# Rotating retention's queries and keys as channels by tokens, and issuing the first attention's scores one slot sooner

## The chip, the cores and the metric

One NeuronCore of a Trainium2 chip. The metric is the time of one execution in microseconds (us). All times of "before" are of the same kernel; lower is better.

## What is computed

One layer of an encoder on 512 tokens of width 1024, in float32: a norm, one projection `h @ w_in`, two mixers side by side, an output projection, a second norm, a router and 16 gated experts, a last norm. What matters here is the second mixer, retention: 4 heads with 128 channels. Its queries and keys are rotated by position and then multiplied with each other:

```python
def rotary(t):                      # t (B,S,H,D)
    half = D // 2
    ang = arange(S)[:, None] * inv[None]
    t1, t2 = t[..., :half], t[..., half:]
    return concatenate([t1 * cos - t2 * sin, t1 * sin + t2 * cos], axis=-1)

qr, kr = rotary(qb), rotary(kb) * 128 ** -0.5
o_b = chunkwise_retention(qr, kr, vb)          # scores need channels on the contracted axis
```

The first mixer is a windowed attention (8 heads of 64 channels, 2 key heads) with a softmax over 192 keys.

## The kernel before, in words

TensorE, VectorE (DVE), ScalarE (ACT), GpSimd (POOL) and the DMA queue SP each run a list of instructions in order; semaphores tie them together.

**Slots.** The projections are a walk over weight groups `g` and tiles `t` (line 74, `STEPS`). Group 0 to 2 give the first attention's queries, keys and values, groups 3 to 10 retention's (3, 4 and 7, 8: queries and keys of a pair of heads; 5, 6 and 9, 10: values and gates), groups 11 to 14 the output projection. A step is called slot `k = (g - 3) * 4 + t`. In each slot TensorE does one tile: 12 matmuls of 512 columns into PSUM bank `t` (`tile_product`, line 1760; every product is a triple of high and low parts, L1577 to L1579). Behind the tile stand small pieces of the mixers, by hand-written slot lists (lines 79 to 94): on TensorE in the order values, transposed probabilities, scores, retention's values, retention's scores, transposes of the rotated tiles (lines 1802 to 1824). ACT and DVE walk the same slots in lists of their own (lines 859 to 914 and 1303 to 1361) and end each slot with a quarter of the split of a weight group that is needed two groups later (L744 or L740 on ACT makes the high part, L1054 or L1049 on DVE the low part).

**First attention.** Eight units `u`, two for each token tile. `scores(u)` (line 1650) writes banks 4 and 5, so for `u` over 0 it waits for `logit_ready` to be `u`: DVE has read the scores of unit `u - 1`. On DVE slot `2u` does, in this order, `softmax_denom(u - 1)` (L1141, L1142, L1144; its last instruction releases `turn_prob(u - 1)`), `attention_out` in some slots (L1151, waits for `values`), `softmax_logits(u)` (L1126 to L1135; its last instruction, L1135, is `logit_ready`). ACT does the exponentials (L806) in slot `2u + 1`, in every case after it has copied the transposed probabilities of unit `u - 1` (L813). TensorE does `scores(u)` in slot `2u`, `turn_prob(u)` (8 transposes, 4 for `u` under 2) in slot `2u + 3` (line 1669), `values` in slots 6, 10, 14, 18.

**Rotation.** Tile `n` (0 to 3 the first pair of heads, 4 to 7 the second) stands in its bank as tokens by channels. `rotate(n)` (line 1153) reads it twice (L1168, L1169: times cosine, times sine) and joins the halves (L1170, L1171) into SBUF; `turn_rot(n)` (line 1694) turns it with 4 transposes on TensorE in slots 6, 8, 10, 12, 22, 23, 25, 26; ACT's `copy_rot(n)` (L817) brings it back into `qkb_t`, channels by tokens. TensorE's tiles of groups 5 and 9 write the same banks again, so tile `t` of group 9 waits for `rot_ready` to be `4 + t + 1` (line 1783). `retention_scores` (L1714), `retention_mask` (L1182, L1185), `retention_values` (L1728) and `retention_out` (L1198 to L1210) follow.

`turn` (L1584) is the helper of all transposes.

Of the kernel before, what the change touches and what calls it, by code (L numbers as in the profile page):

```python
# [17 lines left out]
P = 128  # L18
# [60 lines left out]
TURN_V_SLOT = 1  # L79
SCORE_SLOTS = tuple(range(0, 16, 2))  # L80
DENOM_SLOTS = tuple(range(2, 18, 2))
TURN_SLOTS = tuple(range(3, 19, 2))
VALUE_SLOTS = tuple(range(6, 22, 4))
ROTATE_SLOTS = (5, 7, 7, 9, 20, 22, 23, 25)
ROT_SLOTS = (6, 8, 10, 12, 22, 23, 25, 26)
ROT_BANKS = (7, 7, 7, 7, 5, 6, 5, 6)
RET_SCORE_SLOTS = (18, 20, 27, 29)
# [9 lines left out]
EARLY = 2  # L97
QK_LAST, VG_LAST = (4, 8), (6, 10)
SCM_OFF = (0, 512, 896, 1152)
# [4 lines left out]
def log_gamma(h):  # L104
    return math.log(1.0 - 2.0 ** (-5.0 - h))
# [9 lines left out]
def tile_value(g, t):  # L115

    return STEPS.index((g, t)) + 1 + T if g else t + 1
# [17 lines left out]
def build(nc, x, norm1_g, w_in, attn_sinks, rel_bias, ret_gn_g, w_out, norm2_g, rg_w, rg_b, re_w, re_b,  # L135
          w_gate, w_up, w_down, final_g, table, out):
    ctx = ExitStack()
    with ctx:
# [8 lines left out]
        def sem(name):  # L147
            return ctx.enter_context(nc.semaphore(name))
# [31 lines left out]
        def region(o, n):  # L180
            return arena[:, o:o + n]
# [16 lines left out]
        decay = region(O_DECAY, 1024).rearrange("p (h j) -> p h j", h=B_HEADS)  # L198
        rot = [region(O_ROT, 512), region(O_MIX + 2 * D, 512)]
        rot_b = region(O_TMP, 512)  # L200
        v_t = region(O_ROT, 512)
        cos = region(O_COS, 256).rearrange("p (t c) -> p t c", t=T)
        sin = region(O_COS + 256, 256).rearrange("p (t c) -> p t c", t=T)
        gn_g = region(O_GN, 512)
# [84 lines left out]
        sq_done, root_done, h_ready, h_turned, h_hi, h_lo = (sem(n) for n in ("sq_done", "root_done", "h_ready", "h_turned", "h_hi", "h_lo"))  # L289
        qkv_copied, v_turned, va_copied = sem("qkv_copied"), sem("v_turned"), sem("va_copied")  # L290
        dve_step, act_step = sem("dve_step"), sem("act_step")
# [3 lines left out]
        sink_exp, p_scaled = sem("sink_exp"), sem("p_scaled")  # L295
        rot_ready, rot_turned, rot_copied = sem("rot_ready"), sem("rot_turned"), sem("rot_copied")
        v_copied, gate_copied, silu_done, g_ready = (sem(n) for n in ("v_copied", "gate_copied", "silu_done", "g_ready"))
# [425 lines left out]
        def _(act):  # L723
# [90 lines left out]

            def copy_rot(n):
                act.wait_ge(rot_turned, n + 1)
                nc.scalar.copy(qkb_t[:, :, n % T * P:(n % T + 1) * P],  # L817
                               ps[:, ROT_BANKS[n], :].rearrange("p (b s) -> p b s", b=4)).then_inc(rot_copied, 1)

# [39 lines left out]
            for g, t in STEPS:  # L859
# [11 lines left out]
                if k == TURN_V_SLOT:  # L871
                    act.wait_ge(v_turned, 1)
                    nc.scalar.copy(region(O_VA, 512), ps[:, 7, :]).then_inc(va_copied, 1)
# [12 lines left out]
                if k in MIX_A_SLOTS:  # L886
                    mix_hi(0, [t])
                if k in ROT_SLOTS:
                    copy_rot(ROT_SLOTS.index(k))
                if k in EXP_SLOTS:  # L890
# [143 lines left out]
        def _(dve):  # L1034
# [118 lines left out]
            def rotate(n):  # L1153

                t = n % T
                v = ps[:, t, :].rearrange("p (h a c) -> p h a c", a=2, c=B_DIM // 2)
                own = rot[n % 2 if n < T else 0]
                ra = own.rearrange("p (h a c) -> p h a c", a=2, c=B_DIM // 2)
                rb = rot_b.rearrange("p (h a c) -> p h a c", a=2, c=B_DIM // 2)
                dve.wait_ge(mm_done, tile_value(QK_LAST[n // T], t))  # L1160
                if n:
                    dve.wait_ge(rot_ready, n)
                if n >= 2:
                    dve.wait_ge(rot_turned, n if n >= T else n - 1)
                cs = cos[:, t, :].unsqueeze(1).to_broadcast([P, 8, 64])
                sn = sin[:, t, :].unsqueeze(1).to_broadcast([P, 8, 64])
                v8 = ps[:, t, :].rearrange("p (h c) -> p h c", c=64)
                nc.vector.tensor_tensor(own.rearrange("p (h c) -> p h c", c=64), v8, cs, ALU.mult)  # L1168
                step_done(nc.vector.tensor_tensor(rot_b.rearrange("p (h c) -> p h c", c=64), v8, sn, ALU.mult))  # L1169
                nc.vector.tensor_tensor(ra[:, :, 0, :], ra[:, :, 0, :], rb[:, :, 1, :], ALU.subtract)  # L1170
                nc.vector.tensor_tensor(ra[:, :, 1, :], ra[:, :, 1, :], rb[:, :, 0, :], ALU.add).then_inc(rot_ready, 1)  # L1171

            def retention_mask(i):

                gamma_p = math.exp(log_gamma(i) * P)
                dve.wait_ge(rs_ready, i + 1)
                if i:
                    dve.wait_ge(ro_ready, i)
                for kt in range(T):
                    bank, c0 = ((4, 0), (5, 0), (6, 0), (6, 256))[kt]  # L1180
                    near = min(2, T - kt) * P
                    ins = nc.vector.tensor_tensor(scm[:, SCM_OFF[kt]:SCM_OFF[kt] + near], ps[:, bank, c0:c0 + near],  # L1182
                                                  decay[:, i, 0:near], ALU.mult)
                    for far in range(2, T - kt):
                        ins = nc.vector.scalar_tensor_tensor(  # L1185
                            scm[:, SCM_OFF[kt] + far * P:SCM_OFF[kt] + (far + 1) * P],
                            ps[:, bank, c0 + far * P:c0 + (far + 1) * P], gamma_p ** (far - 1),
                            decay[:, i, P:2 * P], ALU.mult, ALU.mult)
                ins.then_inc(scm_ready, 1)
# [384 lines left out]
        def _(pe):  # L1574
# [89 lines left out]
            def turn_v():  # L1664

                pe.wait_ge(qkv_copied, 8)
                turn(7, [v_t[:, t * P:(t + 1) * P] for t in range(T)]).then_inc(v_turned, 1)

            def turn_prob(u):
                if u:  # L1670
                    pe.wait_ge(pt_copied, probs_value(u - 1))
                if u >= 2:
                    pe.wait_ge(mix_a, u // 2)
                turned = sum(slot < TURN_SLOTS[u] for slot in ROT_SLOTS[:T])
                if turned:
                    pe.wait_ge(rot_copied, turned)
                pe.wait_ge(p_scaled, u + 1)
                for b in range(1 if u < 2 else 0, 2):
                    ins = turn(6 + b, [prob[u % 2][:, hh // 2, hh % 2, b * P:(b + 1) * P] for hh in range(4)])
                ins.then_inc(p_turned, 1)  # L1680
# [12 lines left out]

            def turn_rot(n):
                pe.wait_ge(rot_ready, n + 1)
                if n < T:
                    pe.wait_ge(pt_copied, probs_value(TURN_SLOTS.index(ROT_SLOTS[n] - 1)))
                elif n < T + 2:
                    pe.wait_ge(scm_ready, 2)
                else:  # L1700
                    pe.wait_ge(rot_copied, n - 1)
                own = rot[n % 2 if n < T else 0]
                turn(ROT_BANKS[n], [own[:, i * P:(i + 1) * P] for i in range(4)]).then_inc(rot_turned, 1)

            def retention_scores(i):
                pe.wait_ge(rot_copied, T * (i // 2 + 1))
                if i:
                    pe.wait_ge(scm_ready, i)
                if i == 2:
                    pe.wait_ge(mix_b, 2)  # L1710
                for kt in range(T):
                    bank, c0 = ((4, 0), (5, 0), (6, 0), (6, 256))[kt]
                    n = (T - kt) * P
                    ins = nc.tensor.matmul(ps[:, bank, c0:c0 + n], qkb_t[:, 2 + i % 2, kt * P:(kt + 1) * P],  # L1714
                                           qkb_t[:, i % 2, kt * P:], start=True, stop=True)
                ins.then_inc(rs_ready, 1)
# [43 lines left out]
            def tile_product(g, t):  # L1760
# [17 lines left out]
                else:  # L1778
# [15 lines left out]
                    for k in range(4):  # L1794
                        kk = 4 * half + k
                        ins = triple(ps[:, t, :], ht_hi[:, kk, tok], ht_lo[:, kk, tok],
                                     as_chunks(hi(g))[:, k, :], as_chunks(lo(g))[:, k, :],
                                     half == 0 and k == 0, half == 1 and k == 3)
# [3 lines left out]
            for g, t in STEPS:  # L1802
# [6 lines left out]
                if k in TURN_SLOTS:  # L1809
                    turn_prob(TURN_SLOTS.index(k))  # L1810
                if k in SCORE_SLOTS:
                    scores(SCORE_SLOTS.index(k))
                if k in RET_VALUE_SLOTS:
                    retention_values(RET_VALUE_SLOTS.index(k))
                if k in RET_SCORE_SLOTS:
                    retention_scores(RET_SCORE_SLOTS.index(k))
                if k in ROT_SLOTS:
                    turn_rot(ROT_SLOTS.index(k))
                if k == MIX_B_SLOT:
# [256 lines left out]
```

## Time and profile before

| | us |
|---|---|
| median of 3 runs (548.21 to 549.0) | 548.93 |
| the profiled execution | 548.88 |
| span of its trace | 547.1 |
| TensorE busy in the span | 535.0 (98%) |
| DVE busy in the span | 420.3 (77%) |
| ACT busy in the span | 353.9 (65%) |

The mixers take the stretch from 49 to 192 us of the span; the experts the time from about 247 us to the end. A busy TensorE is not one at its peak: the end of a matmul is modelled, so what tells its pace is the distance from start to start. In rows of the timeline the bracket at the end is idle time ahead of the row and what ended it.

### The profile page before, as it was taken

Reading aid. Unit: us, or ns where it says so; the run is one execution under the profiler, and the core shown is the slowest. Engines: PE = TensorE matmul, PEld = TensorE weight load, DVE = VectorE, ACT = ScalarE, POOL = GpSimd, SP = SyncE. Lnnn points to the kernel's source line nnn. Section 1 sums busy time; section 2 is a strip of 40 time slices with the busy share of each in tenths; the row PEclk is TensorE's granted clock in tenths of the full one; section 3 lists DMA queues with packets and bytes.
Section 4 is the critical chain, followed back from the end, with each engine's and each line's share of the span. In section 5 each row is a group of like instructions: output and inputs, shape, how many; then the busy total and the mean of one; then the engine's idle time right before and its main releaser. Section 6 shows DMA issues by size and latency. Waiting matters only on the chain.

```text
span 547.1 us, 7888 instructions
## 1 busy us (share of the span) xinstructions
PE 535.0 (98%) x2685; PEld 438.7 (80%) x2686; DVE 420.3 (77%) x572; ACT 353.9 (65%) x474; POOL 96.3 (18%) x117
## 2 busy tenths in 40 slices
PE   7999999999999999999999999999999999999994
PEld 5988777777877888898878888888888888888883
DVE  5563599564865853388999889898989898898986
ACT  5563654770226263356877887888787887888745
POOL 3260000000000000034330224122221222110520
PEclk8999999999999999999999999999999999999998
DMA  8999122323020236658999999999999999999894
GB/s 318 374 288 401 44 75 78 77 79 76 2 78 0 78 115 228 236 211 277 399 380 377 373 380 395 375 375 365 381 363 364 373 385 382 371 393 396 264 211 177
DMA packets 63739, 143.78 MB, mean 263 GB/s; under 512 B 3811, under 2 KB 13339, under 8 KB 63584
## 3 DMA queue, kind: packets, MB, share of 16 engines
q1 hardware_dynamic: 56528, 120.24, 61.7%
q0 software_dynamic: 7040, 22.66, 13.5%
q10 hardware_dynamic: 144, 0.52, 0.3%
q8 instruction: 15, 0.25, 0.2%
q14 instruction: 12, 0.10, 0.0%
HBM read 132.51 MB, written 14.30 MB: 268 GB/s over the span
## 4 chain that ended last, share of the span: by engine, by line
PE 88%; DVE 6%; ACT 2%; issue 2%; DMA 1%; ACTq 0%; POOL 0%; DVEq 0%; POOLq 0%
PE ps L1577 25%; PE ps L1579 24%; PE ps L1578 24%; PE ps L1584 7%; DVE lo_ring L1366 2%; PE ps L1728 2%; PE ps L1714 2%; PE ps L1690 1%; PE ps L1660 1%; PE ps L1755 1%; DMA arena<-norm_g 1%; PE ps L1845 1%; DVE act_lo L1064 0%; ACT arena L762 0%; ACT hi_ring L744 0%
## 5 line engine op out<-in xcount | busy, mean ns | idle before, releaser
L1366 DVE TENSOR_TENSOR lo_ring<-arena,hi_ring 128x2048 fp32r<-128x2048 f32 x94 | 213.8, 2288 | 24.7 <-ACT hi_ring L925 24.7
L1577 PE MATMUL ps<-hi_ring,act_hi 128*128 128x512 f32 x576 | 230.0, 399 | 0.3 <-DVE act_lo L1217 0.2
L1579 PE MATMUL ps<-hi_ring,act_lo 128*128 128x512 f32 x576 | 224.9, 390 | 0.0
L1578 PE MATMUL ps<-lo_ring,act_hi 128*128 128x512 f32 x576 | 224.3, 389 | 0.0
L925 ACT ACTIVATE hi_ring<-arena 128x2048 fp32r<-128x2048 f32 x94 | 180.2, 1917 | 26.7 <-PE ps L1579 26.7
L1579 PEld LDWEIGHTS ps<-hi_ring,act_lo 128*128 128x128 f32 x576 | 108.1, 188 | 23.3
L1577 PEld LDWEIGHTS ps<-hi_ring,act_hi 128*128 128x128 f32 x576 | 108.2, 188 | 22.9 <-issue 1.6
L1578 PEld LDWEIGHTS ps<-lo_ring,act_hi 128*128 128x128 f32 x576 | 108.4, 188 | 20.8
L1054 DVE SCALAR_TENSOR_TENSOR lo_ring<-arena,over,hi_ring 128x512 fp32r<-128x512 f32 x40 | 29.3, 748 | 29.4 <-ACT hi_ring L744 29.2
L1064 DVE TENSOR_TENSOR act_lo<-ps,act_hi 128x512 fp32r<-128x512 f32 x56 | 36.8, 683 | 6.4 <-ACT act_hi L777 5.9
L1584 PE MATMUL ps<-keep,arena 128*128 128x128 f32 x260 | 35.2, 275 | 1.2 <-DVE arena L1074 0.7
L631 POOL DMA_INDIRECT arena<-h_dram,gather_idx x12 | 30.9, 2575 | 20.3 <-issue 20.3
L1584 PEld LDWEIGHTS ps<-keep,arena 128*128 128x128 f32 x260 | 29.3, 140 | 5.5 <-issue 1.9
L637 POOL DMA_INDIRECT y_dram<-y,row_info x14 | 15.6, 1112 | 95.1 <-issue 95.1
L561 POOL DMA_DIRECT2D arena<-norm_g x1 | 0.6, 556 | 153.9 <-PE ps L1584 153.9
L744 ACT ACTIVATE hi_ring<-arena,over 128x512 fp32r<-128x512 f32 x40 | 27.5, 718 | 0.1
L1577 PE MATMUL ps<-act_hi,hi_ring 128*128 128x256 f32 (+1 forms) x64 | 22.4, 349 | 0.1
L1579 PE MATMUL ps<-act_hi,lo_ring 128*128 128x256 f32 (+1 forms) x64 | 21.8, 340 | 0.0
L1578 PE MATMUL ps<-act_lo,hi_ring 128*128 128x256 f32 (+1 forms) x64 | 21.8, 340 | 0.0
L945 ACT ACTIVATE act_hi<-ps 128x512 fp32r<-128x512 f32 x15 | 9.0, 601 | 18.7 <-PE ps L1584 18.7
L930 ACT ACTIVATE act_hi<-ps 128x512 fp32r<-128x512 f32 x32 | 17.3, 592 | 5.8 <-PE ps L1845 4.1
L962 ACT ACTIVATE y<-ps,row_info 128x512 f32<-128x512 f32 x28 | 19.0, 679 | 3.1 <-PE ps L1579 3.1
(242 smaller groups left out, 518.4 us busy)
## 6 DMA issues: line engine op xcount, KB each, us to landing
arena<-w_gate SPq DMA_DIRECT2D x32, 1024.0 KB, 16.7
arena<-w_up SPq DMA_DIRECT2D x32, 1024.0 KB, 17.6
arena<-w_down SPq DMA_DIRECT2D x32, 1024.0 KB, 15.2
arena<-w_in SPq DMA_DIRECT2D x16, 512.0 KB, 7.3
y_dram<-arena POOLq DMA_DIRECT2D x8, 512.0 KB, 11.2
res<-y_dram POOLq DMA_DIRECT2D x8, 512.0 KB, 9.7
arena<-w_in SPq DMA_DIRECT2D x2, 1024.0 KB, 10.7
arena<-w_out SPq DMA_DIRECT2D x4, 512.0 KB, 6.4
```

Source lines behind the costliest of these rows:

```text
L631: by_length(e, lambda n: pool.indirect_dma_start(x_rows[b][0:n, :], None, h2_dram, bass.IndirectOffsetOnAxis(ap=gather_idx[0:n, b:b + 1], ...
L744: ins = nc.scalar.activation(dst, src, ACT.Copy, scale=gain)
L925: nc.scalar.activation(hi(N1 + n12), raw(n12), ACT.Copy).then_inc(hi_done, 1)
L930: nc.scalar.activation(xt[b][0][:, 4 * a:4 * a + 4, :], ps[:, 4 + a, :].rearrange("p (k s) -> p k s", k=4), ACT.Copy).then_inc(x_hi, 1)
L962: nc.scalar.activation(y_buf[b][:, a * 512:(a + 1) * 512], ps[:, 2 + a, :], ACT.Copy, scale=row_info[:, 4 * b + 2:4 * b + 3].bitcast(F32)) ...
L1054: ins = nc.vector.scalar_tensor_tensor(dst, src, gain, src_hi.bitcast(F32), ALU.mult, ALU.subtract)
L1064: nc.vector.tensor_tensor(dst, ps[:, bank, :].rearrange("p (k s) -> p k s", k=4), src_hi.bitcast(F32), ALU.subtract).then_inc(done, 1)
L1366: nc.vector.tensor_tensor(lo(N1 + n12), raw(n12), hi(N1 + n12).bitcast(F32), ALU.subtract).then_inc(lo_done, 1)
L1577: nc.tensor.matmul(dst, a_hi, b_hi, start=start, stop=False)
L1578: nc.tensor.matmul(dst, a_hi, b_lo, start=False, stop=False)
L1579: return nc.tensor.matmul(dst, a_lo, b_hi, start=False, stop=stop)
L1584: ins = nc.tensor.transpose(ps[:, bank, i * P:(i + 1) * P], blk, ident)
```

## The change

Weights and activations change roles in groups 3, 4, 7 and 8: bank `t` now holds channel block `t` (two query heads, two key heads) by 512 tokens, so the result needs no transposes. The rotation pairs channel c with c + 64, that is, partitions: ACT copies the two halves of the bank crosswise into SBUF (`swap_halves`), DVE multiplies the bank by a cosine table into `qkb_t`, the swapped copy by a signed sine table, and adds. The tables must stand as channels by tokens: they are turned once on TensorE (`turn_cos`, slot -4) and spread by eight ACT copies; the cosine table moves once (slot 16), because its first place is needed for retention's scores. `turn_rot` and `copy_rot` are gone. TensorE issues `scores(u)` in slots 0, 1, 3, 5, ..., 13, behind the transposes of that slot; the slots of DVE and ACT for the first attention stay.

```diff
 SCORE_SLOTS = tuple(range(0, 16, 2))
+PE_SCORE_SLOTS = (0,) + tuple(range(1, 15, 2))
-ROTATE_SLOTS = (5, 7, 7, 9, 20, 22, 23, 25)
-ROT_SLOTS = (6, 8, 10, 12, 22, 23, 25, 26)
-ROT_BANKS = (7, 7, 7, 7, 5, 6, 5, 6)
+SWAP_SLOTS = (4, 6, 6, 8, 20, 21, 22, 23)
+ROTATE_SLOTS = (5, 7, 7, 9, 21, 22, 23, 25)
+COS_MOVE_SLOT = 16
...
-            def copy_rot(n):
-                act.wait_ge(rot_turned, n + 1)
-                nc.scalar.copy(qkb_t[:, :, n % T * P:(n % T + 1) * P],
-                               ps[:, ROT_BANKS[n], :].rearrange("p (b s) -> p b s", b=4)).then_inc(rot_copied, 1)
+            def spread(f, dst):
+                dims = dst.rearrange("p (i a s) -> p i a s", i=2, a=2)
+                both = ps[:, 6, 2 * f * P:2 * (f + 1) * P].rearrange("p (i s) -> p i s", i=2)
+                for a in range(2):
+                    for half in range(2):
+                        nc.scalar.activation(dims[half * 64:(half + 1) * 64, :, a, :], both[a * 64:(a + 1) * 64, :, :], ACT.Copy,
+                                             scale=-1.0 if f and half == 0 else 1.0).then_inc(cos_set, 1)
+            def swap_halves(n):
+                bank, own = n % T, swap[n % 2]
+                act.wait_ge(mm_done, tile_value(QK_LAST[n // T], bank))
+                if n >= 2:
+                    act.wait_ge(rot_ready, n - 1)
+                for half in range(2):
+                    nc.scalar.copy(own[half * 64:(half + 1) * 64, :],
+                                   ps[(1 - half) * 64:(2 - half) * 64, bank, :]).then_inc(swapped, 1)
...
+                if (g, t) == (NA - 1, 2):
+                    act.wait_ge(rel_out, 16)
+                    act.wait_ge(cos_v_turned, 1)
+                    spread(0, cos_t[0])
+                if k == 0:
+                    spread(1, sin_t)
+                if k == COS_MOVE_SLOT:
+                    act.wait_ge(s_ready, 2 * T)
+                    nc.scalar.copy(cos_t[1], cos_t[0]).then_inc(cos_set, 1)
...
             def rotate(n):
-                dve.wait_ge(mm_done, tile_value(QK_LAST[n // T], t))
...
+                dve.wait_ge(mm_done, tile_value(QK_LAST[pair], block))
+                dve.wait_ge(cos_set, 8 + pair)
+                if pair:
+                    dve.wait_ge(rs_ready, 2)
+                nc.vector.tensor_tensor(turned, ps[:, block, :], cos_t[pair], ALU.mult)
+                dve.wait_ge(swapped, 2 * n + 2)
+                step_done(nc.vector.tensor_tensor(own, own, sin_t, ALU.mult))
+                nc.vector.tensor_tensor(turned, turned, own, ALU.add).then_inc(rot_ready, 1)
...
-            def turn_rot(n):
...
+            def turn_cos():
+                pe.wait_ge(cos_in, 4 * 16)
+                turn(6, [region(O_COS + i * P, P) for i in range(4)]).then_inc(cos_v_turned, 1)
             def retention_scores(i):
-                pe.wait_ge(rot_copied, T * (i // 2 + 1))
+                pe.wait_ge(rot_ready, T * (i // 2 + 1))
...
+                        if g in QK:
+                            ins = triple(ps[:, t, :], as_chunks(hi(g))[:, k, tok], as_chunks(lo(g))[:, k, tok],
+                                         ht_hi[:, kk, :], ht_lo[:, kk, :], half == 0 and k == 0, half == 1 and k == 3)
+                            continue
...
-                if k in SCORE_SLOTS:
-                    scores(SCORE_SLOTS.index(k))
+                if k in PE_SCORE_SLOTS:
+                    scores(PE_SCORE_SLOTS.index(k))
-                if k in ROT_SLOTS:
-                    turn_rot(ROT_SLOTS.index(k))
+                if (g, t) == (NA - 1, 0):
+                    turn_cos()
```

## Rows read from the trace of the kernel before

**Rows 1.** The page, chain of work that ended last, shares by engine

```profile
PE 88%; DVE 6%; ACT 2%; issue 2%; DMA 1%; ACTq 0%; POOL 0%; DVEq 0%; POOLq 0%
```

**Rows 2.** Busy time by stretch: PE, PEld, DVE, ACT, POOL, granted clock, DMA share, GB/s

```profile
49.00:119.00 70.00, 69.76 (x369) 52.44 (x367) 50.82 (x115) 41.12 (x118) 0.00 (x0) 1.00 0.28 86
119.00:192.00 73.00, 72.25 (x362) 57.74 (x363) 47.55 (x129) 23.94 (x45) 0.00 (x0) 1.00 0.19 58
```

**Rows 3.** TensorE's timeline, start, busy us: transposes that go, and tiles around them

```profile
74.25 0.66 PE L1584 MATMUL ps<-keep,arena 128*128 128x128 f32 x4
74.66 0.47 PE L1577 MATMUL ps<-hi_ring,act_hi 128*128 128x512 f32 x1
...
139.55 0.39 PE L1577 MATMUL ps<-hi_ring,act_hi 128*128 128x512 f32 x1
...
142.27 2.39 PE L1728 MATMUL ps<-arena 128*128 128x128 f32 x20
...
153.92 0.66 PE L1584 MATMUL ps<-keep,arena 128*128 128x128 f32 x4 [0.17 <-DVE arena L1171]
154.34 0.47 PE L1577 MATMUL ps<-hi_ring,act_hi 128*128 128x512 f32 x1
```

**Rows 4.** TensorE's timeline, slots 3 to 6, 9, 13: transposes, scores, tiles

```profile
62.50 0.48 PE L1577 MATMUL ps<-hi_ring,act_hi 128*128 128x512 f32 x1
...
65.41 0.92 PE L1660 MATMUL ps<-arena 64*128 64x192 f32 x8
...
69.47 0.47 PE L1577 MATMUL ps<-hi_ring,act_hi 128*128 128x512 f32 x1
...
85.43 1.06 PE L1584 MATMUL ps<-keep,arena 128*128 128x128 f32 x8
86.25 0.48 PE L1577 MATMUL ps<-hi_ring,act_hi 128*128 128x512 f32 x1
...
102.96 1.03 PE L1584 MATMUL ps<-keep,arena 128*128 128x128 f32 x8
```

**Rows 5.** DMA queue and POOL: the last table that turn_cos waits for

```profile
arena<-ret_gn_g POOLq DMA_DIRECT2D x1, 256.0 KB, 8.9
...
18.13 0.54 POOL L540 DMA_DIRECT2D arena<-ret_gn_g  x1
```

**Rows 6.** DVE's timeline: ends of softmax_logits 1, 2, 4, 6, end of softmax_denom 3

```profile
63.85 0.16 DVE L1135 TENSOR_TENSOR norm_tmp<-sinks,norm_tmp 128x4 f32<-128x4 f32 x1
...
70.56 0.16 DVE L1135 TENSOR_TENSOR stat<-sinks,stat 128x4 f32<-128x4 f32 x1
...
84.33 0.96 DVE L1144 TENSOR_TENSOR arena<-arena,norm_tmp 128x768 f32<-128x768 f32 x1
...
87.64 0.17 DVE L1135 TENSOR_TENSOR stat<-sinks,stat 128x4 f32<-128x4 f32 x1
...
104.17 0.16 DVE L1135 TENSOR_TENSOR stat<-sinks,stat 128x4 f32<-128x4 f32 x1
```

**Rows 7.** Groups by shape, 60 to 210 us: busy us, mean ns, idle before

```profile
L1168 DVE TENSOR_TENSOR arena<-ps,arena 128x512 f32<-128x512 f32 x8 | 5.5, 688 | 3.5 <-PE ps L1579 2.3 <-PE ps L1584 1.1
L1170 DVE TENSOR_TENSOR arena<-arena 128x256 f32<-128x256 f32 x8 | 3.4, 426 | 0.3
L1210 DVE TENSOR_TENSOR arena<-arena 128x512 f32<-128x512 f32 x4 | 2.8, 692 | 0.1
```

**Rows 8.** ACT's timeline: two half-height copies out of PSUM, in slot -3

```profile
44.39 1.19 ACT L869 COPY arena<-ps 64x512 f32<-64x512 f32 x2
```

**Rows 9.** DVE's timeline, second pair: the wait for a free bank, and rotate(6)'s end

```profile
145.24 0.69 DVE L1168 TENSOR_TENSOR arena<-ps,arena 128x512 f32<-128x512 f32 x1 [1.13 <-PE ps L1584]
...
153.45 0.42 DVE L1171 TENSOR_TENSOR arena<-arena 128x256 f32<-128x256 f32 x1
```

**Rows 10.** Busy time by stretch at the start, columns as in rows 2

```profile
5.00:10.00 5.00, 3.48 (x15) 2.00 (x15) 3.82 (x9) 3.06 (x6) 0.37 (x1) 0.97 1.04 385
10.00:15.00 5.00, 4.87 (x22) 3.38 (x21) 3.88 (x8) 4.82 (x10) 0.00 (x0) 0.69 1.04 388
```

More of the change, by code:

```diff
@@ L97 @@
 EARLY = 2
-QK_LAST, VG_LAST = (4, 8), (6, 10)
+QK, QK_LAST, VG_LAST = (3, 4, 7, 8), (4, 8), (6, 10)
 SCM_OFF = (0, 512, 896, 1152)
@@ L198, in build @@
         decay = region(O_DECAY, 1024).rearrange("p (h j) -> p h j", h=B_HEADS)
-        rot = [region(O_ROT, 512), region(O_MIX + 2 * D, 512)]
-        rot_b = region(O_TMP, 512)
+        swap = [region(O_ROT, 512), region(O_TMP, 512)]
         v_t = region(O_ROT, 512)
-        cos = region(O_COS, 256).rearrange("p (t c) -> p t c", t=T)
-        sin = region(O_COS + 256, 256).rearrange("p (t c) -> p t c", t=T)
+        cos_t = [region(O_SCM, 512), region(O_QA, 512)]
+        sin_t = region(O_COS, 512)
         gn_g = region(O_GN, 512)
@@ L289, in build @@
         sq_done, root_done, h_ready, h_turned, h_hi, h_lo = (sem(n) for n in ("sq_done", "root_done", "h_ready", "h_turned", "h_hi", "h_lo"))
-        qkv_copied, v_turned, va_copied = sem("qkv_copied"), sem("v_turned"), sem("va_copied")
+        qkv_copied, cos_v_turned, va_copied = sem("qkv_copied"), sem("cos_v_turned"), sem("va_copied")
         dve_step, act_step = sem("dve_step"), sem("act_step")
@@ L295, in build @@
         sink_exp, p_scaled = sem("sink_exp"), sem("p_scaled")
-        rot_ready, rot_turned, rot_copied = sem("rot_ready"), sem("rot_turned"), sem("rot_copied")
+        rot_ready, swapped, cos_set = sem("rot_ready"), sem("swapped"), sem("cos_set")
         v_copied, gate_copied, silu_done, g_ready = (sem(n) for n in ("v_copied", "gate_copied", "silu_done", "g_ready"))
@@ L871, in _ @@
                 if k == TURN_V_SLOT:
-                    act.wait_ge(v_turned, 1)
+                    act.wait_ge(cos_v_turned, 2)
                     nc.scalar.copy(region(O_VA, 512), ps[:, 7, :]).then_inc(va_copied, 1)
@@ L887, in _ @@
                     mix_hi(0, [t])
-                if k in ROT_SLOTS:
-                    copy_rot(ROT_SLOTS.index(k))
+                if (g, t) == (NA - 1, 2):
[7 more added lines that the diff above has]
+                    nc.scalar.copy(cos_t[1], cos_t[0]).then_inc(cos_set, 1)
+                for n, slot in enumerate(SWAP_SLOTS):
+                    if slot == k:
+                        swap_halves(n)
                 if k in EXP_SLOTS:
@@ L1153, in rotate @@
             def rotate(n):
[L1155 to L1159, printed above, removed]
-                dve.wait_ge(mm_done, tile_value(QK_LAST[n // T], t))
[L1161 to L1171, printed above, removed]
+                pair, block = n // T, n % T
+                own, turned = swap[n % 2], qkb_t[:, block, :]
+                dve.wait_ge(mm_done, tile_value(QK_LAST[pair], block))
[6 more added lines that the diff above has]
+                nc.vector.tensor_tensor(turned, turned, own, ALU.add).then_inc(rot_ready, 1)
             def retention_mask(i):
                 gamma_p = math.exp(log_gamma(i) * P)
+                dve.wait_ge(cos_set, 9)
                 dve.wait_ge(rs_ready, i + 1)
@@ L1666, in turn_v @@
                 pe.wait_ge(qkv_copied, 8)
-                turn(7, [v_t[:, t * P:(t + 1) * P] for t in range(T)]).then_inc(v_turned, 1)
+                turn(7, [v_t[:, t * P:(t + 1) * P] for t in range(T)]).then_inc(cos_v_turned, 1)
             def turn_prob(u):
@@ L1673, in turn_prob @@
                     pe.wait_ge(mix_a, u // 2)
-                turned = sum(slot < TURN_SLOTS[u] for slot in ROT_SLOTS[:T])
-                if turned:
-                    pe.wait_ge(rot_copied, turned)
                 pe.wait_ge(p_scaled, u + 1)
@@ L1692, in values @@
                 ins.then_inc(o_ready, 1)
-            def turn_rot(n):
[L1695 to L1703, printed above, removed]
+            def turn_cos():
+                pe.wait_ge(cos_in, 4 * 16)
+                turn(6, [region(O_COS + i * P, P) for i in range(4)]).then_inc(cos_v_turned, 1)
             def retention_scores(i):
-                pe.wait_ge(rot_copied, T * (i // 2 + 1))
+                pe.wait_ge(rot_ready, T * (i // 2 + 1))
                 if i:
@@ L1816, in _ @@
                     retention_scores(RET_SCORE_SLOTS.index(k))
-                if k in ROT_SLOTS:
-                    turn_rot(ROT_SLOTS.index(k))
+                if (g, t) == (NA - 1, 0):
+                    turn_cos()
                 if k == MIX_B_SLOT:
```

## The prediction

> **What bounds the kernel now.** I read the chain of waits first: 88% of it is TensorE, so what TensorE issues or waits for is the time [rows 1]. The table by stretch comes next: in the mixers (49 to 192 us) TensorE is busy 69.8 of 70 us and 72.3 of 73, at full clock, while the DMAs do little (shares of 0.28 and 0.19) [rows 2]. That says that nothing stands ahead of TensorE, but not by how much: DVE is busy 51 of the first 70 us, and it and ACT feed TensorE in each slot. So I read the timelines of both side by side, for how long before its use each result of DVE is there. For a transfer or an engine behind the mixers I found nothing that would absorb a shift: each later load and split waits for a count that TensorE's tiles set, so a microsecond lost or won in the mixers is one at the end. The sum is made against the profiled execution, 548.88 us (span 547.1 and 1.8 around it), and that is within 0.05 of the median, 548.93.
>
> **What leaves and enters TensorE's list.** A tile that nothing interrupts takes 2.72 us from start to start (139.55 to 142.27) [rows 3]. One that follows small pieces and is followed by scores takes 2.91 (62.50 to 65.41) [rows 4], so an interruption costs 0.19 beside its own work. A `turn_rot` takes 0.41 (74.25 to 74.66) [rows 3].
> - First pair: four `turn_rot`, in slots that keep other pieces or lose their scores too: 4 x 0.41 = 1.6 less.
> - Second pair: four `turn_rot`, three of them alone in their slot: 4 x 0.41 + 3 x 0.19 = 2.2 less.
> - Scores in odd slots, which the transposes interrupt anyway: slots 2, 4, 8 and 12 become whole. 4 x 0.19 = 0.8 less. Their own work moves and stays.
> - `turn_cos`: 0.41 and most of an interruption, 0.5 more. It waits for four tables; the last is issued at 18.1 and lands 8.9 us later, at 27 [rows 5], and TensorE comes to it in slot -4, ahead of the copies that ACT makes in slot -3 at 44.4 [rows 8]. So no wait.
> - The query and key tiles with the roles changed: the same number of matmuls of 512 columns and as many weight loads. The nearest rows are the same shape, so 0, with 0.02 a tile either way as bounds.
>
> All of it: 4.1 us less, if TensorE never waits. That is the gain on offer.
>
> **The scores' new wait.** `scores(u)` needs `softmax_logits(u - 1)` finished on DVE. In slot `2u` it had a whole tile more time. Where it stands now is where the next tile starts in the rows, behind the transposes of slot `2u - 1`; I set the end of the logits against it:
> - u = 2: TensorE is there at 62.5 [rows 4], the logits end at 63.85 + 0.16 = 64.0 [rows 6]. 1.5 late.
> - u = 3: 69.5 against 70.7. 1.25 late. u = 5: 86.25 against 87.8. 1.55 late. u = 7: 102.96 + 0.8 = 103.75 against 104.3. 0.6 late [rows 4, 6].
> - u = 1, 4 and 6 read off in the same way come out at 0, 0.2 late and 0.3 early.
>
> These don't add up as they stand: a wait gives DVE time for the next, and a shorter list takes time from it. So I went through slots 1 to 17 in order with the distances of the rows.
> - u = 2: slot 2 is 0.2 shorter, so 1.6 to 1.7 us of wait. Then slot 4 is whole, and TensorE reaches the transposes of slot 5 1.4 later than before. ACT copies these and then does the exponentials, so both are late, by 0.9 net of ACT's own slack, and DVE with them (it has almost no idle time from 66 to 96 us).
> - u = 3: DVE's logits and TensorE are now level: 0.1. u = 4: 0.3.
> - u = 5: `turn_prob(3)` waited for `softmax_denom(3)` already before: it ends at 84.33 + 0.96 = 85.3 and the transposes start at 85.43 [rows 4, 6]. DVE does the logits of unit 4 right behind that denominator, 2.5 us (85.3 to 87.8), and TensorE's transposes take 0.8 (85.43 to 86.25). So whenever DVE is the late one here, the scores wait 2.5 - 0.8 = 1.7. This holds however much the list shrinks.
> - Behind that wait on TensorE stand tile 10 and `values(1)`; DVE's `attention_out(1)` waits for these, and `softmax_logits(5)` for it. So DVE gets about 2 us later, and at u = 7 the wait is 1.3 to 1.4 instead of 0.6.
>
> Together 1.6 + 0.1 + 0.3 + 1.7 + 1.4 and twice 0.1 at the denominators = 5.3 us. Slots 1 to 17 save 1.6 + 0.8 = 2.4 (0.1 more is in gaps that close). Net +2.8 at slot 18. The last wait there, `turn_prob(7)` for its denominator, has no piece that changes and stays.
>
> **The second pair.** `rotate(4)` stood in slot 20 on DVE, in time that was idle; it now needs `retention_scores(1)` done and stands behind `retention_out(0)`. DVE's path from there to the end of `rotate(6)` loses the 1.1 us wait for a free bank [rows 9] and takes in a whole rotation of about 2 us. A rotation itself: before two passes of 0.688 and two of 0.42, after three of 0.69, which is 0.15 less [rows 7]; over three of them 0.4. So `rotate(6)` ends at 153.87 + 2.0 - 1.1 - 0.4 = 154.3. TensorE's tile 26 waits for it, because it writes the bank that `rotate(6)` reads, and before it started at 154.34, behind transposes that had waited for DVE too [rows 3]. So the 2.2 us that TensorE saves turn into a wait at tile 26 (1.7 to 2.0) and tile 27 (0.4). Net 0, I take +0.1.
>
> **ACT.** Eight copies of 0.59 go, sixteen of half height come: a pair takes 1.19 [rows 8], so the height saves nothing and ACT has about 5 us more, with 3 us for the eight spreads (in slots -2 and 0) and 0.6 for the move of the cosine table. The swaps wait for a tile that ACT used to wait for a slot later, and behind them stand only splits that are due two groups on. ACT is busy 41 of 70 us [rows 2]. Cost 0; if the swap of slot 4 pushed the exponentials of slot 5, it would be up to 0.5. The lower bound, that copies freed of `turn_rot` let the exponentials start sooner, is -0.3.
>
> **Sum.** +0.5 (`turn_cos`) + 2.8 + 0.1 = +3.4. 548.9 + 3.4 = 552.3 us. A measurement here can tell about 0.2% (1.1 us) from no change, so this is slower.
>
> **A rule against the change.** At the start TensorE is busy 3.5 of 5 us, and in the 5 us after that the granted clock is 0.69, so some 60% of them passed at the lower of its two levels, which cost 1.5 us [rows 10]. The new waits of 1.4 to 1.7 us stand alone in some 7 us of full work each, so I expect the clock to stay; it is a rival below. The Trainium skill, TensorE: Matmul & The Clock Gate, "Part 1: The HAM clock gate", says that the throttled clock is the default and that activity is what releases it. By that rule the waits could cost more than their length; the rows at the start agree with it, and no row of the mixers shows it.
>
> **The rivals.**
> - *TensorE stays the bound and the transposes' time is won.* Place: `scores(2)` and `scores(5)`, and tile 26. Price: -4.1 if none of them waits, 544.8 us; faster. For it: 98% busy, and 88% of the chain. It decides at the logits: they would have to end 1.6 us sooner, against a DVE list that the change shortens by 0.15 for each rotation only. Against it: rows 6. Chance 0.11.
> - *The first attention's waits are half as long* (ACT freed of copies that waited for `turn_rot`, or a part that I counted twice): +0.5 + 0.1 + 0.2 to 1.0 gives 549.7 to 550.5, and with a gain of 1 us in the second pair 548.7 at the least. Chance 0.14.
> - *The clock falls behind the waits*: once or twice 1.5 us on top, 553.8 to 555. Chance 0.08.
> - *As summed*: 551.2 to 553.4. Chance 0.67.
>
> **How the numbers follow.** The likeliest is 552.3. The range takes in the half-length case from 549.2 and one fall of the clock, 554.0; it leaves out about 0.17. Faster by over 0.2%: the first rival and nearly nothing else, 0.12. Within 0.2% (547.8 to 550.0): most of one half of the second, 0.08. Slower: 0.80.
>
> **What would show it.** After: `scores` rows with an idle bracket that names L1135's line on DVE, some 1.6 us at unit 2, 1.7 at unit 5, 1.4 at unit 7, little at 3, 4 and 6; an idle bracket of nearly 2 us before the third tile of group 9 that names the rotation's last add; slot 18 about 3.3 us later than before, and slot 36 about 3.4; the experts' stretch as long as before. I am wrong if the logits of units 1 and 4 end sooner than here against the transposes, if tile 26 doesn't wait, if rotations take over 2.2 us each (an SBUF add dearer than 0.69), or if granted clocks under 1 appear after 49 us.

## The result: slower by 0.6%, and the profile after

The changed kernel takes 551.74 us (median of 4 runs, 551.45 to 552.32) against 548.57 before (548.13 to 549.0): ratio 1.0058, 95% interval 1.0039 to 1.0077, so 3.2 us more. The profiled execution took 551.84 us, span 550.1.

TensorE's waits from 26 to 215 us of the changed kernel come first (who waited at which line, for whom and whose line: us in total, times, longest). L1678 is `scores`, L1595 the first matmul of a tile, L1602 the transposes; L1159 on DVE is the last instruction of the logits, L1188 the last of a rotation.

```profile
PE ps L1678 <- DVE stat L1159: 2.2, 2, 1.3
PE ps L1595 <- DVE arena L1188: 1.8, 2, 1.7
PE ps L1678 <- DVE norm_tmp L1159: 1.4, 1, 1.4
PE ps L1737 <- issue: 0.5, 1, 0.5
PE ps L1602 <- DVE arena L1168: 0.3, 1, 0.3
```

The first three are new; a sixth, of 0.2, was there before as well. TensorE's timeline of the changed kernel places them (start, busy us; the bracket is idle time ahead of the row):

```profile
40.57 0.60 PE L1602 MATMUL ps<-keep,arena 128*128 128x128 f32 x4
40.92 0.47 PE L1595 MATMUL ps<-act_hi,hi_ring 128*128 128x512 f32 x1
...
52.00 0.71 PE L1678 MATMUL ps<-arena 64*128 64x128 f32 x8
...
62.26 0.65 PE L1602 MATMUL ps<-keep,arena 128*128 128x128 f32 x4
64.33 0.92 PE L1678 MATMUL ps<-arena 64*128 64x192 f32 x8 [1.42 <-DVE norm_tmp L1159]
...
78.95 1.03 PE L1602 MATMUL ps<-keep,arena 128*128 128x128 f32 x8
79.92 0.92 PE L1678 MATMUL ps<-arena 64*128 64x192 f32 x8
...
86.39 1.03 PE L1602 MATMUL ps<-keep,arena 128*128 128x128 f32 x8
88.75 0.92 PE L1678 MATMUL ps<-arena 64*128 64x192 f32 x8 [1.33 <-DVE stat L1159]
...
97.32 1.03 PE L1602 MATMUL ps<-keep,arena 128*128 128x128 f32 x8
...
106.65 0.92 PE L1678 MATMUL ps<-arena 64*128 64x192 f32 x8 [0.86 <-DVE stat L1159]
...
127.66 2.42 PE L1723 MATMUL ps<-arena 128*128 128x512 f32 x8
...
157.50 0.50 PE L1595 MATMUL ps<-hi_ring,act_hi 128*128 128x512 f32 x1 [1.66 <-DVE arena L1188]
160.69 0.50 PE L1595 MATMUL ps<-hi_ring,act_hi 128*128 128x512 f32 x1 [0.17 <-DVE arena L1188]
...
194.96 1.91 PE L1602 MATMUL ps<-keep,arena 128*128 128x128 f32 x16
```

`scores(2)`, `scores(5)` and `scores(7)` wait 1.42, 1.33 and 0.86 us; tile 26, the third of group 9, waits 1.66 and tile 27 0.17. The same places on DVE's timeline:

```profile
60.44 0.75 DVE L1078 SCALAR_TENSOR_TENSOR lo_ring<-arena,over,hi_ring 128x512 fp32r<-128x512 f32 x1 [4.05 <-ACT hi_ring L744]
...
64.02 0.16 DVE L1159 TENSOR_TENSOR norm_tmp<-sinks,norm_tmp 128x4 f32<-128x4 f32 x1
...
85.13 0.96 DVE L1168 TENSOR_TENSOR arena<-arena,norm_tmp 128x768 f32<-128x768 f32 x1
...
88.45 0.16 DVE L1159 TENSOR_TENSOR stat<-sinks,stat 128x4 f32<-128x4 f32 x1
...
94.54 0.69 DVE L1175 COPY arena<-ps 128x512 f32<-128x512 f32 x1 [1.26 <-PE ps L1705]
...
101.97 0.75 DVE L1078 SCALAR_TENSOR_TENSOR lo_ring<-arena,over,hi_ring 128x512 fp32r<-128x512 f32 x1 [3.56 <-ACT hi_ring L744]
...
156.75 0.69 DVE L1188 TENSOR_TENSOR arena<-arena 128x512 f32<-128x512 f32 x1
```

The logits of unit 1 end at 64.18 and `scores(2)` starts at 64.33; those of unit 4 end at 88.61, `scores(5)` starts at 88.75. The denominator of unit 3 (L1168) ends at 86.09 and its logits 2.5 us later, while the transposes between take 0.8. At 94.54 the lateness comes back to DVE: DVE idles 1.26 us for `values(1)`, which stands on TensorE behind the wait at `scores(5)` (these rows answer to [rows 6]). The rows at 60.44 and 101.97 are DVE's shares of the weight splits in slots 1 and 11. Ahead of them DVE idles 4.05 and 3.56 us for ACT, so its list is full ahead of `scores(5)`, but not ahead of `scores(2)` and `scores(7)`.

The mixers fall into two parts, by three marks on TensorE's timeline: start of `scores(0)`, start of `retention_scores(0)` in slot 18, start of the transposes of the mixed rows in slot 35. For the changed kernel these are the rows at 52.00, 127.66 and 194.96; for the other kernels the numbers are read off in the same way.

| kernel | scores(0) | first part, to slot 18 | second part, to slot 35 | span |
|---|---|---|---|---|
| before | 51.83 | 72.86 | 67.16 | 547.1 |
| after | 52.00 | 75.66 | 67.30 | 550.1 |
| scores back | 52.32 | 71.77 | 67.36 | 546.6 |
| scores early alone | 51.91 | 76.32 | 67.14 | 550.4 |
| retention_out(1) later | 55.31 | 75.68 | 64.88 | 551.0 |
| both edits | 51.50 | 71.78 | 64.88 | 543.2 |
| two early | 52.01 | 71.76 | 67.33 | 546.3 |
| less DVE work | 52.10 | 75.32 | 67.31 | 549.8 |

Between before and after the first part has 2.80 us more and the second 0.14. With 0.17 ahead of `scores(0)` and 0.1 less behind slot 35 that is the 3.0 of the spans.

### The profile page after: what moved, and what is told of

The parts are those of the page before. It is cut to its first block, busy times and chain, and to the rows that moved or that the text cites. A ratio compares the mean times of both kernels' runs of the same rounds, so it can differ in the third digit from the quotient of the medians.

```text
span 550.1 us, 7836 instructions
## 1 busy us (share of the span) xinstructions
PE 532.6 (97%) x2657; PEld 436.3 (79%) x2658; DVE 419.6 (76%) x564; ACT 362.9 (66%) x491; POOL 96.5 (18%) x117
## 4 chain that ended last, share of the span: by engine, by line
PE 80%; DVE 11%; ACT 4%; issue 3%; DMA 1%; ACTq 0%; POOL 0%; DVEq 0%; POOLq 0%
PE ps L1595 23%; PE ps L1597 22%; PE ps L1596 22%; PE ps L1602 6%; DVE lo_ring L1384 2%; PE ps L1723 2%; PE ps L1737 1%; ACT arena L806 1%; PE ps L1764 1%; PE ps L1705 1%; DMA arena<-norm_g 1%; PE ps L1858 1%; DVE lo_ring L1078 1%; DVE arena L1185 1%; DVE arena L1150 1%
## 5 line engine op out<-in xcount | busy, mean ns | idle before, releaser
L1595 PE MATMUL ps<-hi_ring,act_hi 128*128 128x512 f32 x512 | 204.0, 398 | 2.1 <-DVE arena L1188 1.8
L1597 PE MATMUL ps<-hi_ring,act_lo 128*128 128x512 f32 x512 | 199.9, 390 | 0.0
L1596 PE MATMUL ps<-lo_ring,act_hi 128*128 128x512 f32 x512 | 199.5, 390 | 0.0
L1595 PEld LDWEIGHTS ps<-hi_ring,act_hi 128*128 128x128 f32 x512 | 96.2, 188 | 25.6 <-issue 3.7
L1596 PEld LDWEIGHTS ps<-lo_ring,act_hi 128*128 128x128 f32 x512 | 96.3, 188 | 18.8
L1595 PE MATMUL ps<-act_hi,hi_ring 128*128 128x512 f32 (+1 forms) x128 | 48.0, 375 | 0.1
L1597 PE MATMUL ps<-act_hi,lo_ring 128*128 128x512 f32 (+1 forms) x128 | 46.5, 363 | 0.0
L1596 PE MATMUL ps<-act_lo,hi_ring 128*128 128x512 f32 (+1 forms) x128 | 46.5, 363 | 0.0
L1602 PE MATMUL ps<-keep,arena 128*128 128x128 f32 x232 | 31.2, 278 | 0.8 <-DVE arena L1098 0.5
L1602 PEld LDWEIGHTS ps<-keep,arena 128*128 128x128 f32 x232 | 27.0, 143 | 3.3 <-DVE arena L1098 0.9
L1595 PEld LDWEIGHTS ps<-act_hi,hi_ring 128*128 128x128 f32 x128 | 24.1, 189 | 6.3 <-issue 1.8
L1597 PEld LDWEIGHTS ps<-act_hi,lo_ring 128*128 128x128 f32 x128 | 24.1, 188 | 3.9
L1596 PEld LDWEIGHTS ps<-act_lo,hi_ring 128*128 128x128 f32 x128 | 24.2, 189 | 3.4
```

What stands on the lines that cost most here:

```text
L1595: nc.tensor.matmul(dst, a_hi, b_hi, start=start, stop=False)
L1596: nc.tensor.matmul(dst, a_hi, b_lo, start=False, stop=False)
L1597: return nc.tensor.matmul(dst, a_lo, b_hi, start=False, stop=stop)
L1602: ins = nc.tensor.transpose(ps[:, bank, i * P:(i + 1) * P], blk, ident)
```

## The experiments

**Scores back.** One line of the changed kernel; TensorE's scores stand in the even slots again.

```diff
-PE_SCORE_SLOTS = (0,) + tuple(range(1, 15, 2))
+PE_SCORE_SLOTS = SCORE_SLOTS
```

> The changed kernel with the first attention's scores back in TensorE's slots 0, 2, ..., 14. Theory (the loss is TensorE waiting at scores(2), scores(5) and scores(7) for DVE's logits of the unit before): these waits (1.4 + 1.3 + 0.9 us) and the 0.2 us ahead of scores behind transposes go, four interruptions of 0.2 come back, and the first pair's 1.6 us of transposes show, but for a wait of about 0.6 at turn_prob(3): 3.3 to 3.8 us less than the changed kernel, 547.9 to 548.5, level with the kernel before (ratio 0.999). The waits at tile 26 and 27 stay. Rival (the rotation's new list on DVE and ACT makes the loss, wherever the wait shows): the waits move to the transposed probabilities, and it stays over 550.5.

Measured: 547.8 us (10 runs) against 548.66 for the kernel before, of which there were 19 runs beside these experiments (ratio 0.9983, 0.9974 to 0.9993). The first part is 3.9 us shorter than in the changed kernel, and its waits are these (columns as above):

```profile
PE ps L1595 <- DVE arena L1188: 1.9, 2, 1.7
PE ps L1602 <- DVE arena L1168: 0.7, 2, 0.4
PE ps L1737 <- issue: 0.5, 1, 0.5
PE ps L1595 <- DVE act_lo L1235: 0.2, 1, 0.2
```

No score waits. The wait at `turn_prob(3)` that the theory wanted is the 0.4 in the second row; the other 0.3 in it is `turn_prob(7)`. The waits did not move elsewhere, so the rival falls, and the time is slightly below the range that I gave. So the rotation alone is a small gain, 0.9 us.

**Scores early alone.** The other half: the kernel before, with the scores moved and nothing else.

```diff
+PE_SCORE_SLOTS = (0,) + tuple(range(1, 15, 2))
...
-                if k in SCORE_SLOTS:
-                    scores(SCORE_SLOTS.index(k))
+                if k in PE_SCORE_SLOTS:
+                    scores(PE_SCORE_SLOTS.index(k))
```

> The kernel before with nothing changed but TensorE's scores in slots 0, 1, 3, ..., 13. Theory: waits of 1.4 to 1.6 us at scores(2), 0.9 to 1.3 at scores(5), 0.6 at scores(7), each kept to the end: 2.9 to 3.3 us slower than before, 551.5 to 551.9. Rival (the rotation makes the loss): 548 to 549, as before, or up to 0.5 faster for the interruptions saved.

Measured: 552.23 us (ratio 1.0065, 1.0048 to 1.0082), 3.6 us more than before, nearly all of it in the first part (+3.46). The loss is there without the new rotation, so the rival falls. But 552.23 is above the range that I gave, while the waits at `scores(5)` and `scores(7)`, 0.79 and 0.40, are shorter than I expected.

```profile
PE ps L1661 <- DVE norm_tmp L1136: 1.4, 1, 1.4
PE ps L1661 <- DVE stat L1136: 1.2, 2, 0.8
```

The idle time at the scores is 2.6 us, less than the 3.46. One reason is a gap that I had not priced: scores behind transposes start 0.17 to 0.18 us after the transposes would let a tile start. It shows at 78.95 in the changed kernel: eight transposes take 0.79 when a tile follows (115.22 to 116.01 in the changed kernel; 0.82 from 85.43 to 86.25 before [rows 4]), and 0.97 when scores do (78.95 to 79.92). The other reason is that a bracket starts at the modelled end of the transposes, 0.24 to 0.3 us behind the point where a tile would start. Counted from that point, TensorE loses 1.72, 1.02 and 0.65 us at units 2, 5 and 7, and 0.17 or 0.18 at each of the other four, 4.1 in all. Two interruptions saved (slots 2 and 4) are 0.4, and slots 8 and 12, where `turn_rot` still stands, give 0.1 each: 4.1 - 0.6 = 3.5. So the move would lose something even where DVE is on time: the gap is paid at each of the seven units, and a whole tile is won only at those that leave slot 2, 4, 8 or 12. Units 3, 5 and 7 leave slots that `values` interrupts anyway.

**retention_out(1) later.** For the second part: in the changed kernel DVE and ACT do it behind `rotate(7)`, which itself comes one slot sooner.

```diff
-ROTATE_SLOTS = (5, 7, 7, 9, 21, 22, 23, 25)
+ROTATE_SLOTS = (5, 7, 7, 9, 21, 22, 23, 24)
+RET_OUT_SLOTS = (20, 24, 31, 32)
...
-                if k in RET_VALUE_SLOTS:
-                    retention_out(RET_VALUE_SLOTS.index(k))
+                if k in RET_OUT_SLOTS:
+                    retention_out(RET_OUT_SLOTS.index(k))
```

(and the same for ACT's root in that step)

> The changed kernel with DVE's and ACT's share of retention_out(1) in slot 24 instead of 22, behind rotate(7), which moves from slot 25 to 24. Theory (in the second pair DVE's list between rotate(4) and rotate(7) is what tiles 26 and 27 wait for, and it hides what TensorE saves): both waits go, 1.7 + 0.2 of idle time and the lead-in ahead of it: 2.0 to 2.4 us less than the changed kernel, 549.3 to 549.7. Rival (the second pair's saving is eaten by something else, such as ACT's swaps): tile 26 still waits, now for a rotation that waits for a swap, and it gains under 0.7.

Measured: 549.62 us (11 runs), ratio 1.0015 (1.0005 to 1.0025), 2.1 us less than the changed kernel's 551.74, as expected. The second part is 64.88 instead of 67.30, 2.4 shorter, and no tile waits for a rotation. The first part is the changed kernel's to 0.02 us. The span of this execution is longer all the same, and the table shows why: `scores(0)` came 3.3 us later, for the reason told in the last section.

**Both edits.** The two edits stand in one kernel: scores back, and `retention_out(1)` later.

> Both edits: scores back in the even slots, and retention_out(1) behind rotate(7). Theory: the gains add, since one lies in slots 2 to 14 and the other in 22 to 27: 5.4 to 6.2 us less than the changed kernel, 545.5 to 546.3, which is 2.3 to 3.0 less than before (ratio 0.995). Rival (the stretch behind gives it back, the experts being bound by their weights): 547.5 or more.

Measured: 545.4 us (544.99 to 545.75), ratio 0.994 (0.9923 to 0.9956): 6.3 us less than the changed kernel and 3.3 less than the 548.66 of before. So the new rotation gains 3.3 us when the scores stay where they were and DVE does this one step later. The two parts are those of the two experiments alone, 71.78 and 64.88. What still waits:

```profile
PE ps L1603 <- DVE arena L1169: 0.7, 2, 0.4
PE ps L1738 <- issue: 0.5, 1, 0.5
PE ps L1596 <- DVE act_lo L1236: 0.2, 1, 0.2
```

The span is 3.9 us shorter than before, of which the two parts are 3.4 and the start is 0.3, so the stretch of the experts gives nothing back. The time is 0.1 below my range; the early part of this execution ran at full clock (last section), but the median of four runs is below the range as well.

**Two early.** Only units 1 and 6 stand early.

```diff
+PE_SCORE_SLOTS = (0, 1, 4, 6, 8, 10, 11, 14)
```

> The changed kernel with scores in TensorE's slots 0, 1, 4, 6, 8, 10, 11, 14: only units 1 and 6 stand early, where the logits of the unit before should be ready. Theory (an early place costs only where DVE is late): no wait at scores(1), at most 0.3 at scores(6). Beside the kernel with all scores back, two interruptions of 0.2 go and two gaps of 0.2 between transposes and scores come, so the mixers end within 0.3 us of its end. Rival (an early place costs by itself, for what stands behind it): it is slower by 0.5 or more for these two.

One run, 548.15 us beside one of 548.17 for the kernel before. The first part takes 71.76, as with all scores back (71.77). Nothing waits at a score:

```profile
94.62 1.03 PE L1602 MATMUL ps<-keep,arena 128*128 128x128 f32 x8
95.61 0.92 PE L1678 MATMUL ps<-arena 64*128 64x192 f32 x8
```

From 94.62 to 95.61 is 0.99, the 0.8 of the transposes and the gap. An early place costs nothing where DVE is on time and gains nothing either, for these two units: each leaves a slot (2 and 12) that becomes whole, and that pays for the gap.

**Less DVE work.** `rotate(1)` and `rotate(2)` end after their first product; the sine part of these two tiles is left out.

```diff
+                if n in (1, 2):
+                    first.then_inc(rot_ready, 1)
+                    return
```

> The changed kernel with rotate(1) and rotate(2) cut to their first product on DVE (the sine part of these two tiles is left out), 2.6 us of work between logits 3 and denominator 3. Theory (scores(5) waits for DVE's list, which runs without idle time up to it): TensorE's wait at scores(5) shrinks from 1.3 to between 0.5 and 1.0, not by the whole 2.6, because behind the first half microsecond DVE waits for ACT's split and exponentials instead; scores(2) waits as long as before (1.4), since it lies ahead of the cut. Rival (the wait is for the order of denominator and logits alone, whatever the load): 1.3 stays.

One run, 551.51 us; the first part 75.32.

```profile
64.43 0.92 PE L1681 MATMUL ps<-arena 64*128 64x192 f32 x8 [1.42 <-DVE norm_tmp L1159]
...
88.51 0.92 PE L1681 MATMUL ps<-arena 64*128 64x192 f32 x8 [0.95 <-DVE stat L1159]
```

DVE's timeline, its share of the split in slot 7:

```profile
83.82 0.75 DVE L1078 SCALAR_TENSOR_TENSOR lo_ring<-arena,over,hi_ring 128x512 fp32r<-128x512 f32 x1 [2.17 <-ACT hi_ring L744]
```

`scores(5)` waits 0.95 instead of 1.33, `scores(2)` 1.42 as before. So DVE's load counts, but 2.6 us of it less gave 0.4: now DVE idles 2.17 us for ACT, which makes the high part of the split behind the transposes of slot 7 and its exponentials. That loop is what is left of the wait, as expected. This bears on the first rival of the prediction: even a DVE list much shorter than this one would not have ended the wait at unit 5.

## Why the prediction was right

It gave 552.3 us, 549.2 to 554.0; measured were 551.84 for the profiled execution and 551.74 for the median. Point by point:

- *Second pair's and first pair's transposes, 1.6 and 2.2 less.* The 1.6 is what "scores back" shows (the changed list of transposes without the move of the scores): 72.86 - 1.6 and a wait of 0.4 to 0.5 at `turn_prob(3)` is 71.7, measured 71.77. The 2.2 shows in "retention_out(1) later": 67.16 to 64.88, 2.3 less.
- *`turn_cos` 0.5, no wait.* The transposes take 0.35 (40.57 to 40.92) and the first matmuls behind them run 0.1 late. There is no idle bracket. The mark at 52.00 is only 0.17 later, because in this execution the unbroken run of tiles ahead of these transposes began 0.3 us sooner (at 23.98, before at 24.28).
- *The scores' waits, 5.3.* This was the step that carried the sign, and it held in place: units 2, 5 and 7 wait, each for DVE's logits. What the scores moved on TensorE's list, counted from where the transposes would let a tile start: 1.71 at unit 2 (62.62 to 64.33), 1.57 at unit 5 (87.18 to 88.75), 1.11 at unit 7, and 0.17 or 0.18 at each of units 1, 3, 4 and 6: 5.1 in all. I had 1.6, 1.7, 1.4, 0.4 for units 3 and 4, and 0.2 at the denominators.
- *Unit 7, the reason.* It was sized 0.3 too long, by a step that failed. I let DVE's lateness behind `values(1)` run on to `softmax_logits(6)`. But DVE has idle time between the two, and had it before, so the lateness ends there:

```profile
99.79 0.75 DVE L1054 SCALAR_TENSOR_TENSOR lo_ring<-arena,over,hi_ring 128x512 fp32r<-128x512 f32 x1 [3.53 <-ACT hi_ring L744]
```

The chain that sets unit 7 starts on TensorE, with the transposes of slot 11: ACT copies them, does the exponentials of unit 5 and the high part of the split, and only then does DVE go on to the split, `softmax_denom(5)` and `softmax_logits(6)`. From the start of these transposes to the end of the logits it is 9.18 us before (95.15 to 104.33) and 9.18 in the changed kernel (97.32 to 106.50). TensorE's own way to the end of the transposes of slot 13 fell from 8.60 to 8.22, and that makes the wait longer.
- *Unit 2, the reason.* DVE idles 4.05 us ahead of its split in slot 1 (row at 60.44), for ACT, and on ACT's way there, ahead of the first exponential, stands a table load of 1.28 us, at 56.75 as it stood at 56.58 before:

```profile
56.58 1.28 ACT L806 ACT_TABLE_LOAD   x1
```

So less work on DVE ahead of these two idle times would not have made the logits of unit 1 or 6 sooner; this is read from the rows, except that "less DVE work" left unit 7 as it was (0.87). No run moved the table load, so what it is worth at `scores(2)` is not shown.
- *Interruptions, 0.8 less.* These were priced without the gap between transposes and scores, 0.7 at units 1, 3, 4 and 6. In its place stood 0.6 of waits that did not come: the rows of these units have no bracket, and the only wait at a denominator, 0.3 at `turn_prob(7)`, was there before. That the first part came out at +2.80, as forecast, is therefore luck in part. One term stood for the other, and what TensorE lost at the scores (5.1 for 5.3) and what it saved (2.3 for 2.5) were each 0.2 less than in the sum.
- *Second pair, 0 to +0.1, tile 26 waiting 1.7 to 2.0 and tile 27 0.4.* Measured +0.14, 1.66 and 0.17. The last add of `rotate(6)` ends at 157.44, 29.78 after the mark in slot 18; before, `rotate(6)` ended at 153.87 [rows 9], 29.18 after it, and tile 26 starts 29.84 after the mark instead of 29.65.
- *A rotation, 0.15 less on DVE.* Its three passes take 2.05 against 2.21 (the sum of their means):

```profile
L1188 DVE TENSOR_TENSOR arena<-arena 128x512 f32<-128x512 f32 x8 | 5.5, 692 | 0.3
L1185 DVE TENSOR_TENSOR arena<-ps,arena 128x512 f32<-128x512 f32 x8 | 5.5, 682 | 0.0
L1187 DVE TENSOR_TENSOR arena<-arena 128x512 f32<-128x512 f32 x8 | 5.4, 680 | 0.0
```

- *ACT, 0.* It has 9 us more of busy time (362.9 against 353.9) and no wait of TensorE or DVE names one of its new lines. Its copy of half height takes 582 ns, one of full height 587 (L813, 128x512):

```profile
L831 ACT COPY arena<-ps 64x512 f32<-64x512 f32 x16 | 9.3, 582 | 13.9 <-PE ps L1597 11.1 <-DVE arena L1188 2.4
```

- *The rivals.* TensorE bound throughout: fell, since three scores and tile 26 have idle brackets. Half the waits: fell, they were 5.1 of the 5.3. The clock did not fall behind the waits: the granted clock from 27 to 192 us was 1.00 in every profile of the study, so waits of up to 1.7 us in this stretch did not lower it, and no run tests there what the Trainium skill, TensorE: Matmul & The Clock Gate, "Part 1: The HAM clock gate", says of a throttled default that activity releases. The start agrees with it only in part: the clock of before fell to 0.69 behind five us in which TensorE was busy 3.48 us, and was 1.00 again in the five behind [rows 10]. But "both edits" had 3.44 us busy in the same stretch and stayed at 1.00, and the first five us were at 1.00 in every profile.

Shown by experiment are the causes of the first part's loss (two kernels, one for each half of the change) and of the second part's missing gain (tile 26's wait taken away by order alone). Shown at unit 5 are the share of DVE's load, 0.4, and that DVE then idles for ACT. That ACT's loop sets units 2 and 7 is read from the timelines and was not tested by an edit. What makes the 0.18 us gap stays open: no run changed the kind of matmul behind transposes.

## What to carry to other kernels

Before an instruction that frees or fills a buffer is moved sooner on the bound engine, put the end of what it waits for against its new place for every repetition, not for one: here three of seven were late by over a microsecond, and nothing behind them gave it back. Ask too which chain makes the result late: at two of the three it was idle time of DVE for ACT, which DVE's busy time doesn't tell. An engine at 98% does not mean that work taken from it is time won; in the second pair DVE ended under half a microsecond ahead of TensorE's tile, and a change of order on that engine (one step moved behind four short ones) was worth 2.4 us of that stretch. And a change of two parts is worth trying in halves: one half was -0.9 us, the other +3.6.

## What I had not expected of the hardware

The scores, matmuls on 64 rows, start about 0.18 us late behind fp32 transposes on 128 (0.97 for eight transposes and gap, in both kernels that have all scores early), while tiles of 128 rows follow them at once (0.79 to 0.82). Behind a tile, scores start 0.09 late (0.32 from 51.68 to 52.00, where the matmuls of a tile have 0.23).

The start of a program differs from execution to execution by more than many changes are worth. In the stretches from 10 to 15 and from 15 to 20 us the granted clock of TensorE was 0.69 and 1.00 in the profile of before (its first value in [rows 10]); the rows of "retention_out(1) later" and, behind them, of "both edits" for the same stretch (PE, PEld, DVE, ACT, POOL busy, granted clock, DMA share, GB/s) are:

```profile
10.00:15.00 5.00, 4.87 (x19) 3.78 (x18) 3.62 (x7) 4.31 (x9) 0.00 (x0) 0.50 1.04 396
15.00:20.00 5.00, 5.00 (x23) 3.98 (x22) 1.96 (x4) 0.79 (x2) 3.10 (x6) 0.57 1.09 348
```

```profile
10.00:15.00 5.00, 4.28 (x28) 3.13 (x28) 4.22 (x9) 4.91 (x10) 0.12 (x1) 1.00 1.04 389
15.00:20.00 5.00, 5.00 (x45) 5.00 (x45) 2.52 (x4) 1.71 (x4) 3.34 (x6) 1.00 1.09 349
```

At 0.50 and 0.57 nearly all of the stretch passed at the lower of the two levels (1.2 GHz), at 1.00 none of it, and `scores(0)` starts at 55.31 in the one and at 51.50 in the other, though the two kernels are the same up to there. Who compares two profiles should subtract a mark behind the start, as the table does, ahead of reading anything into their spans.
